# VectorE's remainders as scalar-tensor-tensor operations, banks dealt out anew, and two output products interleaved, in a feed-forward layer of seven block products

## What is computed

```
def swiglu(x, w_gu, w_down):
    g, u = jnp.split(x @ w_gu, 2, axis=-1)
    return (jax.nn.silu(g) * u) @ w_down
...
        u = modulate(rmsnorm(h, norm3_g[l]), mod[:, 2, 0], mod[:, 2, 1])
        h = h + FFN_RES_WEIGHT * mod[:, 2, 2][:, None, :] * swiglu(u, ffn2_w_gu[l], ffn2_w_down[l])
```

## Time and profile before

| | |
|---|---|
| runs | 2051.27 us (2049.93 to 2052.34) |
| profiled execution | 2052.13 us, span 2050.6 us |
| TensorE (PE) busy | 2010.1 us, 98% |
| VectorE (DVE) busy | 1197.6 us, 58% |
| ScalarE (ACT) busy | 890.9 us, 43% |
| GpSimd (POOL) busy | 372.4 us, 18% |
| the layer, in the span | plain chunks from about 762 us, block products from 789 us, the last part's output products until about 1115 us |

### The profile page before, as it was taken

The page is one execution under the profiler, slowest core; times in us unless marked ns, Lnnn a source line. Parts: engine busy times, 40 slices in busy tenths (PEclk is TensorE's granted clock), DMA queues, the critical chain, the costliest instruction groups (busy, mean ns, idle before and its releaser), DMA issues.

```text
span 2050.6 us, 25835 instructions
## 1 busy us (share of the span) xinstructions
PE 2010.1 (98%) x10133; PEld 1713.6 (84%) x10133; DVE 1197.6 (58%) x1721; ACT 890.9 (43%) x1282; POOL 372.4 (18%) x261
## 2 busy tenths in 40 slices
PE   7999999999999998999999999999999999999998
PEld 6888888888888888899897888888888888888888
DVE  6665655624555667568486445544476475564666
ACT  5322223436665554345255455554434343342444
POOL 5000000001101223122120344443000021020130
PEclk8999999999999999999999999999999999999999
DMA  8755663532223522324232433333544333333232
GB/s 314 273 188 193 195 196 110 176 93 82 74 84 110 185 93 84 123 73 124 83 99 97 145 119 104 113 117 104 195 124 143 124 103 95 101 93 103 80 112 77
DMA packets 84393, 261.42 MB, mean 127 GB/s; under 512 B 9248, under 2 KB 13472, under 8 KB 84272
## 3 DMA queue, kind: packets, MB, share of 16 engines
q1 hardware_dynamic: 84272, 259.77, 39.6%
HBM read 242.92 MB, written 16.81 MB: 127 GB/s over the span
## 4 chain that ended last, share of the span: by engine, by line
PE 90%; DVE 5%; ACT 3%; issue 1%; DMA 0%; POOL 0%; SPq 0%; DVEq 0%; ACTq 0%; POOLq 0%
PE P L900 29%; PE P L902 28%; PE P L901 28%; PE P L1120 1%; PE P L1397 1%; PE P L1132 1%; DVE WL L763 1%; PE P L1131 1%; DVE SB L2699 1%; ACT WH L749 0%; PE P L1013 0%; DVE SQ L2282 0%; DVE TL L2653 0%; PE P L1444 0%; DVE SL L2575 0%
## 5 line engine op out<-in xcount | busy, mean ns | idle before, releaser
L900 PE MATMUL P<-UH,WH 128*128 128x512 f32 (+1 forms) x1687 | 640.9, 380 | 13.4 <-DVE SIL L2367 7.2
L902 PE MATMUL P<-UH,WL 128*128 128x512 f32 (+1 forms) x1687 | 636.4, 377 | 0.0
L901 PE MATMUL P<-UL,WH 128*128 128x512 f32 (+1 forms) x1687 | 636.3, 377 | 0.0
L749 ACT ACTIVATE WH<-WRAW 128x1024 fp32r<-128x1024 f32 (+2 forms) x324 | 330.7, 1026 | 600.1 <-PE P L902 596.5
L763 DVE TENSOR_TENSOR WL<-WRAW,WH 128x1024 fp32r<-128x1024 f32 (+2 forms) x265 | 332.5, 1257 | 135.4 <-ACT WH L749 134.8
L900 PEld LDWEIGHTS P<-UH,WH 128*128 128x128 f32 x1687 | 319.4, 189 | 72.5 <-DVE SIL L2367 7.6
L902 PEld LDWEIGHTS P<-UH,WL 128*128 128x128 f32 x1687 | 319.2, 189 | 58.3
L901 PEld LDWEIGHTS P<-UL,WH 128*128 128x128 f32 x1687 | 319.4, 189 | 56.0
L778 POOL TENSOR_TENSOR WL<-WRAW,WH 128x1024 fp32r<-128x1024 f32 x59 | 143.8, 2438 | 349.3 <-ACT WH L749 349.3
L900 PE MATMUL P<-AH,WH 128*128 128x512 f32 x500 | 195.5, 391 | 3.4 <-DVE AL L2747 3.4
L901 PE MATMUL P<-AL,WH 128*128 128x512 f32 x500 | 194.8, 390 | 0.0
(11 more groups left out here) (328 smaller groups left out, 3227.3 us busy)
## 6 DMA issues: line engine op xcount, KB each, us to landing
WRAW<-w_gu SPq DMA_DIRECT2D x88, 512.0 KB, 3.6
ADA<-w_ada SPq DMA_DIRECT2D x72, 512.0 KB, 4.7
WRAW<-w_down SPq DMA_DIRECT2D x48, 512.0 KB, 3.6
WRAW<-w_up SPq DMA_DIRECT2D x44, 512.0 KB, 3.5
WRAW<-w_in SPq DMA_DIRECT2D x40, 512.0 KB, 3.6
WRAW<-w_mix SPq DMA_DIRECT2D x36, 512.0 KB, 3.6
WRAW<-w_down SPq DMA_DIRECT2D x24, 384.0 KB, 3.1
WRAW<-w_out SPq DMA_DIRECT2D x16, 512.0 KB, 3.9
```

The source lines that it names most:

```text
L749: s.act.activation(hi, self.raw(item), FN.Copy).then_inc(*self.rounded.inc(item))
L900: pe.matmul(out, wh, xh, start=start, stop=False, skip_group_check=True)
L901: pe.matmul(out, wh, xl, start=False, stop=False, skip_group_check=True)
L902: return pe.matmul(out, wl, xh, start=False, stop=stop, skip_group_check=True)
```

## The change

Four edits, all in this layer:

1. VectorE's remainders and sums are written as `scalar_tensor_tensor(out, a, 1.0, b, mult, subtract)`, (a x 1.0) - b, where they were `tensor_tensor(out, a, b, subtract)`: the weights' low parts from up(1) to the item before the last part's first output product, the token sums' TL, the two sums SB, and the remainder AL.
2. Banks: m1, m2 and m5 have 5, 0, 1 for even f and 2, 3, 4 for odd f. The output products have 6, 5, 0, 1, 3, 4, 2, 3. The next layer's banks start one later. All other banks stand.
3. In VectorE's loop glu(f-1) stands ahead of the sums of f+1, and no longer behind them.
4. At a part's end output product 1 is opened before product 0 is closed: product 0 up to the last but one tile, product 1 up to the last but one, then the last tile of each. To fit, the high and low part of product 1's weights are made after snap m7 and after c22, no longer ahead of them.

```
+    def beside_pool(self, item):
+        return self.at_item[self.at["ffn2", "up", 1]] <= self.at_item[item] < \
+            self.at_item[self.at["ffn2", "down", 2, 0]]
...
+            if self.beside_pool(item):
+                s.dve.scalar_tensor_tensor(lo, self.raw(item), 1.0, hi.bitcast(F32), OP.mult,
+                                           OP.subtract).then_inc(*self.low_v.inc(item))
+                continue
             s.dve.tensor_tensor(lo, self.raw(item), hi.bitcast(F32), OP.subtract).then_inc(
...
-        for x, b in (("m1", 0), ("m2", 2), ("m5", 4)):
-            plan["ffn2", x, f] = b + f % 2
+        for x, b in zip(("m1", "m2", "m5"), (2, 3, 4) if f % 2 else (5, 0, 1)):
+            plan["ffn2", x, f] = b
     for p in range(3):
-        for m, b in enumerate((6, 2, 3, 4, 5, 0, 1, 3)):
+        for m, b in enumerate((6, 5, 0, 1, 3, 4, 2, 3)):
             plan["ffn2", "down", p, m] = b
-    at = 4
+    at = 5
...
-    def down(tiles):
+    def down(m, tiles):
...
         else:
-            down(range(3))
+            down(0, range(3))
         m4(f)
         m3(f)
-    down(range(3, nf))
+
+    down(0, range(3, nf - 1))
+    down(1, range(nf - 1))
+    down(0, range(nf - 1, nf))
+    down(1, range(nf - 1, nf))
...
-        for m in range(1, KD):
+        for m in range(2, KD):
...
@@ act_quads, last f of a part
         else:
-            W.round(later[1])
             snap("m7", f, U2)
             W.round(later[2])
...
-    dve.tensor_tensor(mem.SB[:, LEFT:RIGHT], up[:, RIGHT:D], mem.SA[:, RIGHT:D],
-                      OP.subtract).then_inc(*s.comb.inc("s2", f))
+    dve.scalar_tensor_tensor(mem.SB[:, LEFT:RIGHT], up[:, RIGHT:D], 1.0, mem.SA[:, RIGHT:D],
+                             OP.mult, OP.subtract).then_inc(*s.comb.inc("s2", f))
...
@@ dve_quads
         W.low(W.up(f))
+        if f != fs[0]:
+            glu(f - 1)
         if f != fs[-1]:
             dve_sums(s, f + 1)
         if f != fs[0]:
-            glu(f - 1)
             lower(f - 1)
...
-            W.low(later[1])
             c22(f)
             W.low(later[2])
```

More of the change, by code:

```diff
@@ L1284, in m3 @@
         s.drained[bank("m5", f)] = [s.comb("c12", f)]
-    def down(tiles):
-        tag = ("ffn2", "down", p, 0)
+    def down(m, tiles):
+        tag = ("ffn2", "down", p, m)
         b, (wh, wl) = s.bank[tag], W.parts(W.at[tag])
@@ L1299, in down @@
             last.then_inc(*W.done.inc(W.at[tag]))
-            s.drained[b] = [s.resid("ffn2", p, 0)]
+            s.drained[b] = [s.resid("ffn2", p, m)]
     m1(fs[0])
@@ L2652, in form @@
         on.wait_ge(*s.snap("t hi", t))
-        dve.tensor_tensor(mem.TL[:, t - 1], mem.form(t), mem.TH[:, t - 1].bitcast(F32),
-                          OP.subtract).then_inc(*s.comb.inc("t lo", t))
+        dve.scalar_tensor_tensor(mem.TL[:, t - 1], mem.form(t), 1.0,
+                                 mem.TH[:, t - 1].bitcast(F32), OP.mult, OP.subtract).then_inc(*s.comb.inc("t lo", t))
     def glu(e, f):
@@ L2698, in dve_sums @@
     on.wait_ge(*W.loaded[W.up(f) % 4](W.up(f)))
-    dve.tensor_tensor(mem.SB[:, LEFT:RIGHT], up[:, RIGHT:D], mem.SA[:, RIGHT:D],
-                      OP.subtract).then_inc(*s.comb.inc("s2", f))
+    dve.scalar_tensor_tensor(mem.SB[:, LEFT:RIGHT], up[:, RIGHT:D], 1.0, mem.SA[:, RIGHT:D],
+                             OP.mult, OP.subtract).then_inc(*s.comb.inc("s2", f))
     on.wait_ge(*s.comb("s2", f))
-    dve.tensor_tensor(mem.SB[:, RIGHT:D], gate[:, RIGHT:D], mem.SB[:, LEFT:RIGHT],
-                      OP.subtract).then_inc(*s.comb.inc("s4", f))
+    dve.scalar_tensor_tensor(mem.SB[:, RIGHT:D], gate[:, RIGHT:D], 1.0, mem.SB[:, LEFT:RIGHT],
+                             OP.mult, OP.subtract).then_inc(*s.comb.inc("s4", f))
 def dve_quads(s, p):
@@ L2746, in lower @@
         on.wait_ge(*s.a_hi("ffn2", f))
-        dve.tensor_tensor(mem.AL2[:, j, :], mem.SIL2[:, f % 2, :], mem.AH2[:, j, :].bitcast(F32),
-                          OP.subtract).then_inc(*s.a_lo.inc("ffn2", f))
+        dve.scalar_tensor_tensor(mem.AL2[:, j, :], mem.SIL2[:, f % 2, :], 1.0,
+                                 mem.AH2[:, j, :].bitcast(F32), OP.mult, OP.subtract).then_inc(*s.a_lo.inc("ffn2", f))
     W.low(W.gate(fs[0] + 1))
```

## The result

The changed kernel takes 2042.51 us (median of five runs, 2041.51 to 2042.72), the kernel before 2051.27 us (five runs, 2049.93 to 2053.60). The ratio is 0.9954, with a 95% interval of 0.9940 to 0.9969. Forecast were 2041.3 us, in a range of 2038.5 to 2046.5. The profiled execution took 2042.68 us, with a span of 2041.4.

A forecast was written before the change was run, and what follows sets the result against it. TensorE, 98% busy, was taken as the bound. Part ends, loop and start, -5.8 - 3.2 - 1.0 = -10.0 us, took the profiled 2052.13 us to 2042.1, an expected median of 2041.3 us; range 2038.5 to 2046.5.

The forecast's parts named there:

- Part ends: At the three parts' ends: interleaving products 0 and 1 removes the waits for AL and the clock's dip, -5.8 us.
- Loop: In the loop: glu ends 1.5 us earlier where 0.42 are needed, so seven late starts of m1 go, -3.2 us.
- The new form: On VectorE: each scalar-tensor-tensor costs 0.06 us more, 0.42 us a round, 9.65 of 10.08 us; no cost on TensorE.
- Start: Start of the block products: m1 and m2 of quad 3 run earlier, the wait moves behind m2; -1.0 us.
- A: In the loop: VectorE mildly becomes the bound, the seven stalls stay as other waits; 2044.5 us, chance 0.12.
- B: At the layer's start: the clock stays up, or other waits vanish; 2039.6 us, chance 0.08.
- C: At the part ends: nothing gained, because product 1's weights are late; 2047.1 us, chance 0.05.
- E: Whole layer: nothing of note, two of the three terms fail; about 2048 to 2051 us, chance 0.04.
- D: In the loop: GpSimd's first sum beats gate's low part, 1.25 us more each VectorE round; 2057.5 us, chance 0.05.

The follow-up runs named there:

- e2: The kernel before with only output products 0 and 1 interleaved at the parts' ends, product 1's weights prepared later: 2046.54 us.
- e4: The kernel before with the new banks alone: 2050.09 us.
- e3: The kernel before with only glu(f-1) moved ahead of the two sums in VectorE's loop: 2049.68 us.
- e5: The changed kernel with the new scalar-tensor-tensors multiplying by a per-partition column of ones in SBUF in place of the immediate 1.0: 2043.39 us.
- e1: The changed kernel with every new scalar-tensor-tensor put back to a tensor-tensor; banks, glu's place and interleaved products stay: 2043.10 us.
- e8: The changed kernel with three further scalar-tensor-tensors of 320 columns ahead of VectorE's sums in each of 16 loop rounds: 2053.11 us.

## Why the prediction was right, and where it was not

**Part ends, 5.8 us: right.** Measured 5.9 in the stages and 6.1 us alone (e2). The weights of product 1 were not late: no wait is left at any end, and the granted clock is 1.00 there. What the prediction took for certain, the dip of the clock behind 2.04 us of waiting, is not: e4 had the wait without the dip. That the kernel before had it in its profile is luck for 1.6 of the 5.9 us.

**Loop, 3.2 us: right.** Measured 3.1 in the stages and 3.0 us alone (e3).

**The new form, +0.06 us each: wrong.** The row it came from the earlier trace rows is an operation whose scalar is a column in SBUF, and e5 shows the column to be the price: 1.28 us with it, 1.22 without. The expected 9.65 us of VectorE's round were 9.1 (9.03 in 10 us), and nothing in the time hung on it. The Trainium skill ("VectorE: DVE Perf Modes", the section on the TRN2 errata) has (N + 151) / 0.96 ns for a float32 tensor-tensor, which is 1.22 us for 1024 columns, an estimate from its formula. The trace agrees for both forms, with 1.22 us each. The prediction should have doubted whether its row was of the same form.

**Start, 1.0 us: mis-sized, measured 2.0.** The mechanism was right: m1 and m2 move up, and the wait stands behind them on the copy of m1(3). m1 came 0.77 us behind the last plain matmul (expected 1.16), and m6(3) 9.51 us behind it, where it was 12.87. TensorE lost 0.54 us ahead of m1 and 5.79 behind m2, where 0.9 and 6.1 were expected: 0.7 us less. The price of the new form, which did not come, explains 0.4 of it and not the 0.7 us of the forecast: e5, where it is paid, loses 0.74 and 5.98 us, 0.4 more than the changed kernel. So less than 11 prices reached m6(3) even there; why was not measured. The last 0.3 us between 1.0 and 2.0 lie in the slow phase, and that belongs to the execution, not to the kernel. Counted as distances of about 0.21 us, it had 25 in the kernel before, 26 in e3 and 17 in e2, whose starts are the same program; and 15 in the changed kernel, 27 in e1, 13 in e4, 15 in e5, 18 in e8, with one and the same long wait of 5.6 to 5.8 us. At 0.09 us each this moves the start by up to 1.3 us from one profile to the next. So of the 2.0 us 1.0 is shorter waiting (7.36 - 6.33), and the rest is within what two profiles of one program differ by.

**Rivals.** A did not come: no gap in the loop. Nor did B: the clock fell. C is excluded by e2, E by the stages, in which all three terms came. D's mechanism did come, in every round with sums of GpSimd: its first sum got in ahead of the low part of gate, which took 1.91 to 2.20 us. The price it was given, 1.25 us on top, was wrong, since its other side was named ("out of the sums' way") but not set against it: in the round shown the low part loses 0.95 us, and VectorE's first sum gains 1.1, as GpSimd is through earlier. So the argument against D held, but that it would outweigh D was not reckoned, and that was luck. There was some room: in e5 VectorE's round was 0.3 us over TensorE's 10.08 and cost nothing.

**The median.** The stages sum to 11.0 us in the layer, and the medians are 8.8 us apart, with an interval of 6.4 to 12.3 us. For the kernels of the table the two are 10.0 and 9.6 us (e1), 6.8 and 6.1 (e2), 3.2 and 3.0 (e3), 3.8 and 2.6 (e4). The dips of the clock, at the start and at the third end, are in some profiles and not in others, and one pair of profiles shows one draw of them. Whether this is the whole of the difference was not measured. That the median came within 1.2 us of the forecast is in part luck: the layer gained 1.0 us more than forecast, and the medians show 2.2 us less than the layer.

## What to carry over

Read a loss of TensorE as distances of starts, stage by stage, and take each wait's end from the order of the engine that ends it: the largest wait left was for one copy that stood behind three operations which the next product did not need, and moving it up shortened the layer by 3.1 us more, 1.7 of it waiting and the rest the clock. When a row prices an operation, compare all its operands with those of the new one, the scalar included. Where two engines contend, sum what the loser loses and what the next operation gains, over a whole round, and ask how far an engine may fall behind before anyone waits.

## What the runs showed of the hardware

- A scalar-tensor-tensor with an immediate takes as long as a tensor-tensor (1.22 us at 1024 columns, 0.68 at 512, float32 in SBUF); with a per-partition column 0.06 us more (1.28, 0.74).
- Beside GpSimd it is delayed as a tensor-tensor is: 1.91 to 2.20 us for 1.22 in the changed kernel, and 1.91 to 2.20 us with tensor-tensors in e1 and e3.
- Behind one and the same wait of 2.04 us TensorE's granted clock fell to 0.50 in two kernels and stayed at 1.00 in a third; with a wait of 5.6 to 5.8 us (five kernels) it fell each time, for 13 to 27 slow matmuls, and in the changed kernel before the wait was over. After two waits of 1.72 and 1.30 us it stayed at 1.00.
